# Two transformer blocks in one kernel: the square sum of the differential heads as two rounded matmuls, issued behind other matmul work

## The chip, the cores and the metric

The kernel runs on one core of one Trainium2 chip. The metric is the device time of one execution in microseconds (us), as the median of repeated runs. The profile is one execution, taken by the hardware profiler. Engines: PE (matmuls, with PEld for the load of their weights), DVE (vector), ACT (scalar), POOL (GpSimd) and SP (it issues the transfers).

## The reference

The whole is one convolution-and-attention block, followed by one block with two kinds of attention over 512 tokens of width 1024. The change lies in the second block, in the normalization of its differential heads (4 heads of width 128):

```
p = jax.nn.softmax(sc, axis=-1)
a = p[:, :, 0] - lam * p[:, :, 1]
d_out = einsum(a, dv)                                            # per head: 512 tokens x 128
d_out = rms_norm(d_out, diff_subln) * (1.0 - lambda_init)        # mean of squares over the head's 128 values
d_out = d_out * jax.nn.silu(dg)
mixed = jnp.concatenate([m_out, d_out], axis=-1)
x = x + jnp.einsum('bse,ed->bsd', mixed, w_out)
```

The other heads (`m_out`, 8 heads of width 64, handled in pairs) have a block-sparse attention of their own, which with 512 tokens is causal over all keys.

## The kernel before

Each engine has an instruction stream of its own, written out by hand in program order; semaphores join them (`wait_ge` on one side, `then_inc` on the other). An engine works through its stream in that order, so what stands behind a waiting instruction waits too.

**Precision.** A product of two fp32 matrices is done as three matmuls of rounded parts (`products`: high by high, low by high, high by low; type fp32r). ACT writes a high part, DVE or POOL the low part, which is the value minus its high part. A matmul on plain fp32 operands stands in the trace as two records, each with a weight load of its own.

**The second attention** goes over eight chunks c = 0 to 7: even ones are differential heads, odd ones are pairs of the other heads. The loop over c = 0, 2, 4, 6 interleaves the stages of c, c + 1, c + 2 and c + 3 so that PE always has projections of later chunks between the attention steps. Stages that matter here:

- `value_half(c, half)`: half of a value projection, 12 matmuls of 512 columns (L463 to L465), into PSUM bank 7. For c of 3 and more its first half waits for `v2_lo_ready`, which counts the low parts of values: `value_half(c + 3, 0)` may overwrite bank 7 only after `value_low(c + 2)` (DVE, tile `vd_lo` for an even chunk) has read it. That one waits for `stage_v2(c + 2)` on ACT (tile `vd_hi`).
- `square_out(c)` (ACT, L1537): the squares of the raw differential head, tile `d_sq`, in plain fp32.
- `square_sum(c)` (PE, L1013 and L1015): the sum of `d_sq` over the 128 values by a matmul with a matrix of ones, and then four fp32 matmuls of 128 columns that add the term for epsilon (tile `rx_d`). The result, in the output bank, is read by `variance(c)` (DVE, tile `d_v`).
- `low_probs(c + 1, 0)` (DVE, tile `pt_lo`): the low part of the transposed probabilities, 1280 columns. It reads the transposes' bank. The next ten transposes, `transposes(c + 1, 1)` (PE, L952), wait for it (`ptl_ready`), since they overwrite that bank.
- `scores2(c + 2, 0)` (PE, L928): scores of the next differential head.

In DVE's stream `value_low(c + 2)`, `variance(c)` and `low_probs(c + 1, 0)` stand one behind the other. In PE's stream the order for c = 0, 2 and 4 is: ten transposes of chunk c + 1, `square_sum(c)`, `value_half(c + 3, 0)`, `scores2(c + 2, 0)`, ten more transposes. For c = 6 the square sum is followed by `out_chunks(0, 0, 6)`, 18 matmuls of the output projection, and then by the ten transposes `transposes(7, 1)`. So the square sum stands in the program four times.

Of the kernel before, what the change touches and what calls it, by code (L numbers as in the profile page):

```python
# [8 lines left out]
F32R = mybir.dt.float32r  # L9
BF16 = mybir.dt.bfloat16  # L10
ALU = mybir.AluOpType
ACT = mybir.ActivationFunctionType
AX = mybir.AxisListType

P = 128
T = 512
D = 1024
KC = D // P
# [62 lines left out]
def two_layer_block(nc, xT, vecs, wstream, outT):  # L81
    with ExitStack() as ctx:
        at = {}
# [11 lines left out]
        def sem(name):  # L95
            return ctx.enter_context(nc.semaphore(name))
# [120 lines left out]
        s2 = put("s2", [P, 2, 1280], F32)  # L217
        v_t = put("v_t", [P, T], F32)
        d_v = put("d_v", [P, T], F32)
        rx_d = put("rx_d", [P, TB, P], F32)  # L220
        rx_m = put("rx_m", [P, TB, P], F32)
        pt_hi = put("pt_hi", [P, 1280], F32R)
# [24 lines left out]
        def out_weights(t):  # L247
# [47 lines left out]
        out_read, raw_copied, dsq_ready, dss_ready, dvar_ready, drs_ready, d_final, att2_final, mixed_ready = (  # L295
            sem("out_read"), sem("raw_copied"), sem("dsq_ready"), sem("dss_ready"), sem("dvar_ready"),
            sem("drs_ready"), sem("d_final"), sem("att2_final"), sem("mixed_ready"))
        pool_held, gap_zeroed = sem("pool_held"), sem("gap_zeroed")
        first_done, first_sq, first_acc, first_drained = (
            sem("first_done"), sem("first_sq"), sem("first_acc"), sem("first_drained"))  # L300
# [159 lines left out]
        def _(pe):  # L460
# [421 lines left out]
            def value_half(c, half):  # L882

                if c >= KC:
                    return
                n = v_unit(c)
                if half == 0:
                    if c < 2:
                        pe.wait_ge(tile_drained, CREDIT + T_Q2 + 15 + c)
                    elif c == 2:  # L890
                        pe.wait_ge(g_drained, 1)
                    else:
                        pe.wait_ge(v2_lo_ready, c)
                    pe.wait_ge(lo_ready, n + 1)
                for k in range(4 * half, 4 * half + 4):
                    w = slice(k * P, (k + 1) * P)
                    mm = products(ps[:, v_bank(c), :], w_hi[:, n % 2, w], w_lo[:, n % 2, w], a_hi[:, k, :], a_lo[:, k, :],
                                  first=k == 0, last=k == KC - 1)
                if half:
                    mm.then_inc(units_done, 1)  # L900
# [32 lines left out]
            def transposes(c, head=0):  # L933

                if c >= KC:
                    return
                tq = tq_of(c, head)
                if tq == 0:
                    pe.wait_ge(nb_used, 16)
                if is_diff(c):  # L940
                    pe.wait_ge(p2_joined, c // 2 + 1)
                    if c:
                        pe.wait_ge(row2_used, c // 2)
                else:
                    pe.wait_ge(p2_exp, 2 * c + head + 1)
                if tq:
                    pe.wait_ge(ptl_ready, tq)
                for j in range(TB):
                    for b in range(j, TB):
                        src = S_COL[b] + j * P  # L950
                        o = PT_BANK * 512 + P_COL[j] + (b - j) * P
                        mm = pe.transpose(psf[:, o:o + P], s2[:, head, src:src + P], ident[:, :])  # L952
                mm.then_inc(pt_ready, 1)
# [53 lines left out]
            def square_sum(c):  # L1007

                if c >= KC:
                    return  # L1010
                pe.wait_ge(dsq_ready, c // 2 + 1)
                pe.wait_ge(rx_ready, c + 1)
                pe.matmul(ps[:, OUT_BANK, :], ones[:, :], d_sq[:, :], start=True, stop=False, skip_group_check=True)  # L1013
                for b in range(TB):
                    mm = pe.matmul(ps[:, OUT_BANK, b * P:(b + 1) * P], rx_d[:, b, :], ident[:, :], start=False,  # L1015
                                   stop=b == TB - 1, skip_group_check=True)
                mm.then_inc(dss_ready, 1)

            def out_chunks(t, first, last):

                high, low = out_weights(t)
                if first == 0:
                    pe.wait_ge(lo_ready, U_W2 + t + 1)
                for n in range(first, last):
                    pe.wait_ge(mixed_ready, n + 1)
                    j = W2_ORDER[n]
                    w = slice(j * P, (j + 1) * P)
                    mm = products(ps[:, W2_BANKS[t], :], high[:, w], low[:, w], b_hi[:, j, :], b_lo[:, j, :],
                                  first=n == 0, last=n == KC - 1)
                if last == KC:  # L1030
                    mm.then_inc(units_done, 1)
# [34 lines left out]
            for c in range(0, KC, 2):  # L1066
                transposes(c)
                if c:
                    value_transposes(c + 1)
                scores2(c + 1, 0)  # L1070
                if 0 < c < KC - 2:
                    value_half(c + 2, 0)
                    value_half(c + 2, 1)
                    scores2(c + 1, 1)
                    gate_half(c + 1, 0)
                    scores2(c + 1, 2)
                    gate_half(c + 1, 1)
                else:
                    gate_half(c + 1, 0)
                    scores2(c + 1, 1)  # L1080
                    gate_half(c + 1, 1)
                    scores2(c + 1, 2)
                values2(c)
                value_transposes(c + 2)
                transposes(c + 1, 0)
                if c + 2 < KC:
                    square_sum(c)
                    value_half(c + 3, 0)
                    scores2(c + 2, 0)
                    transposes(c + 1, 1)  # L1090
                    scores2(c + 2, 1)
                    value_half(c + 3, 1)
                    scores2(c + 2, 2)
                    values2(c + 1, 0)
                    gate_part(c + 2, 0, 5)
                    values2(c + 1, 1)
                    den_rows(c + 1)
                    gate_part(c + 2, 5, KC)

            square_sum(KC - 2)  # L1100
            pe.wait_ge(g_drained, KC)
            out_chunks(0, 0, KC - 2)
            transposes(KC - 1, 1)
            values2(KC - 1, 0)
            pe.wait_ge(s2_biased, 4 * 16)
# [15 lines left out]
        def _(act):  # L1121
# [412 lines left out]
            def square_out(c):  # L1534

                act.wait_ge(raw_copied, c // 2 + 1)
                act.activation(d_sq[:, :], att2[:, 0, :], ACT.Square).then_inc(dsq_ready, 1)  # L1537

            def first_root(c):
# [110 lines left out]
        def _(dve):  # L1650
# [497 lines left out]
            def value_low(c):  # L2148

                if c >= KC:  # L2150
                    return
                dve.wait_ge(v2_hi_ready, c + 1)
                src = ps[:, v_bank(c), :].rearrange("p (b f) -> p b f", f=P)
                if is_diff(c):
                    low(vd_lo[:, :, :], src, vd_hi[:, :, :]).then_inc(v2_lo_ready, 1)
                else:
                    low(by_heads(v2_lo[:, :, :])[:, :, 0:3:2, :], by_heads(src), by_heads(v2_hi[:, :, :])[:, :, 0:3:2, :]
                        ).then_inc(v2_lo_ready, 1)
# [102 lines left out]
            def raw_out(c):  # L2261
# [5 lines left out]
                    dve.wait_ge(mixed_ready, c - 1)  # L2267
                dve.tensor_copy(att2[:, 0, :], ps[:, OUT_BANK, :]).then_inc(raw_copied, 1)

            def variance(c):  # L2270

                dve.wait_ge(dss_ready, c // 2 + 1)
                ts(d_v[:, :], ps[:, OUT_BANK, :], 1.0 / P, ALU.mult).then_inc(dvar_ready, 1)
# [44 lines left out]
            for c in range(0, KC, 2):  # L2318
                biased(c + 1, 0)
                low_probs(c)  # L2320
                if c:
                    value_drain(c + 2)
                den_small(c)
                den_spread(c)
                biased(c + 1, 1)
                if 0 < c < KC - 2:
                    biased(c + 1, 2)
                    gate2_drain(c + 1)
                else:
                    gate2_drain(c + 1)  # L2330
                    biased(c + 1, 2)
                raw_out(c)
                den_small(c + 1)
                den_spread(c + 1)
                slopes(c + 2)
                value_low(c + 2)
                variance(c)
                low_probs(c + 1, 0)
                biased(c + 2, 0)
                biased(c + 2, 1)  # L2340
                value_drain(c + 3)
                root(c)
                biased(c + 2, 2)
                low_probs(c + 1, 1)
                joined(c + 2, (3, 2, 0, 1))
                gate_row(c + 1)
                gate2_drain(c + 2)
                slopes(c + 3)
                value_low(c + 3)
                if c + 2 < KC:  # L2350
                    gated(c + 1)
# [355 lines left out]
```

## Time and profile before

| what | value |
|---|---|
| median of three runs | 1017.15 us (1017.1 to 1017.25) |
| the profiled execution's own time | 1017.32 us |
| span of the profiled execution | 1015.2 us |
| PE busy | 1002.7 us, 99% of the span |
| DVE, ACT, POOL busy | 557.7, 454.0, 502.3 us |
| granted clock of PE, mean | 1.0 |

The span runs from the first to the last instruction in the profile; 2.1 us of the execution lie around it. Matmul records overlap, since a matmul's record runs on while the next one is started: the distance from start to start is what one costs PE. A row of the timeline can stand for several like instructions (x10).

### The profile page before, as it was taken

How to read it: one execution, taken by the hardware profiler on the slowest of the kernel's cores; microseconds unless marked ns; L12 is line 12 of the kernel's file. 1: busy time of each engine (PE TensorE's matmuls, PEld its weight loads, DVE VectorE, ACT ScalarE, POOL GpSimd, SP SyncE). 2: the span in 40 equal slices, each digit the busy share in tenths (PEclk: the TensorE clock that was granted, in tenths of full speed). 3: DMA queues.
4: the chain of work that ended last, by engine and by line, in shares of the span. 5: the costliest groups of instructions: out<-in, count | busy, mean ns of one | idle time of the engine just before them, and what ended most of it. 6: DMA issues, size and time to landing. Idle time of an engine off the chain costs nothing.

```text
span 1015.2 us, 13705 instructions
## 1 busy us (share of the span) xinstructions
PE 1002.7 (99%) x5051; PEld 836.2 (82%) x5051; DVE 557.7 (55%) x943; ACT 454.0 (45%) x682; POOL 502.3 (49%) x296
## 2 busy tenths in 40 slices
PE   9999999999999999999999999999999999999998
PEld 7888888788888988888888888889988778777787
DVE  6799897886633964434434410116714276675731
ACT  7222346888643533323323322233554347667630
POOL 4444365742347034444444365453377544755562
PEclk9999999999999999999999999999999999999999
DMA  7232222212144022222322333333132120111112
GB/s 258 83 104 97 92 83 71 75 63 83 65 184 146 21 93 94 103 92 94 103 92 94 103 104 104 104 122 107 43 104 82 63 84 22 64 63 43 42 63 83
DMA packets 26402, 91.11 MB, mean 90 GB/s; under 512 B 3056, under 2 KB 3184, under 8 KB 26224
## 3 DMA queue, kind: packets, MB, share of 16 engines
q1 hardware_dynamic: 26352, 90.42, 26.2%
q8 instruction: 34, 0.56, 0.2%
q14 instruction: 16, 0.13, 0.0%
HBM read 88.31 MB, written 2.10 MB: 89 GB/s over the span
## 4 chain that ended last, share of the span: by engine, by line
PE 87%; DVE 7%; ACT 3%; issue 1%; DMA 1%; POOL 0%; SPq 0%; DVEq 0%; ACTq 0%
PE ps L463 27%; PE ps L464 26%; PE ps L465 26%; PE ps L928 2%; PE ps L952 1%; DVE resid L2015 1%; PE ps L622 1%; DVE a_lo L1666 1%; DMA w_raw<-weights 1%; DVE sq_x L1659 1%; DVE q_raw L1659 1%; DVE mix L1659 1%; DVE b_lo L1666 1%; ACT s L1510 0%; PE ps L638 0%
## 5 line engine op out<-in xcount | busy, mean ns | idle before, releaser
L2363 POOL TENSOR_TENSOR w_lo<-w_raw,w_hi 128x1024 fp32r<-128x1024 f32 x137 | 325.9, 2379 | 412.0 <-ACT w_hi L1129 359.2
L1129 ACT ACTIVATE w_hi<-w_raw 128x1024 fp32r<-128x1024 f32 x133 | 139.2, 1046 | 281.6 <-PE ps L465 281.6
L463 PE MATMUL ps<-a_hi,w_hi 128*128 128x512 f32 (+1 forms) x544 | 211.7, 389 | 4.2 <-DVE v_lo L1663 3.1
L465 PE MATMUL ps<-a_hi,w_lo 128*128 128x512 f32 (+1 forms) x544 | 207.0, 380 | 0.0
L464 PE MATMUL ps<-a_lo,w_hi 128*128 128x512 f32 (+1 forms) x544 | 206.9, 380 | 0.0
L463 PE MATMUL ps<-b_hi,w_hi 128*128 128x512 f32 x392 | 152.9, 390 | 0.0
L465 PE MATMUL ps<-b_hi,w_lo 128*128 128x512 f32 x392 | 152.6, 389 | 0.0
L464 PE MATMUL ps<-b_lo,w_hi 128*128 128x512 f32 x392 | 152.5, 389 | 0.0
L463 PEld LDWEIGHTS ps<-a_hi,w_hi 128*128 128x128 f32 x544 | 102.3, 188 | 27.3 <-DVE v_lo L1663 4.4
L465 PEld LDWEIGHTS ps<-a_hi,w_lo 128*128 128x128 f32 x544 | 102.3, 188 | 20.0
L464 PEld LDWEIGHTS ps<-a_lo,w_hi 128*128 128x128 f32 x544 | 102.4, 188 | 18.3 <-issue 0.2
L463 PEld LDWEIGHTS ps<-b_hi,w_hi 128*128 128x128 f32 x392 | 73.6, 188 | 15.2
L465 PEld LDWEIGHTS ps<-b_hi,w_lo 128*128 128x128 f32 x392 | 73.6, 188 | 15.2
L464 PEld LDWEIGHTS ps<-b_lo,w_hi 128*128 128x128 f32 x392 | 73.6, 188 | 15.1
L1743 DVE SCALAR_TENSOR_TENSOR ps<-u_pad,vec,ps 128x512 f32<-128x512 f32 x112 | 75.4, 750 | 0.0
L463 PE MATMUL ps<-h_hi,w_hi 128*128 128x512 f32 (+1 forms) x186 | 69.2, 372 | 0.0
L464 PE MATMUL ps<-h_lo,w_hi 128*128 128x512 f32 (+1 forms) x186 | 69.0, 371 | 0.0
L465 PE MATMUL ps<-h_hi,w_lo 128*128 128x512 f32 (+1 forms) x186 | 69.0, 371 | 0.0
L1659 DVE TENSOR_TENSOR up_h<-up_u,up_s 128x512 f32<-128x512 f32 x22 | 51.2, 2330 | 21.2 <-ACT up_s L1389 21.1
L1659 DVE TENSOR_TENSOR up_u<-ps,scale_row 128x512 f32<-128x512 f32 x22 | 15.2, 690 | 82.0 <-PE ps L465 82.0
L1659 DVE TENSOR_TENSOR sq_f<-sq_f 128x512 f32<-128x512 f32 x13 | 12.5, 960 | 82.7 <-ACT sq_f L1413 82.0
L1510 ACT ACTIVATE s<-s,smax 128x384 f32<-128x384 f32 (+2 forms) x64 | 35.2, 552 | 16.9 <-DVE smax L2188 16.9
(339 smaller groups left out, 1729.0 us busy)
## 6 DMA issues: line engine op xcount, KB each, us to landing
w_raw<-weights SPq DMA_DIRECT2D x156, 512.0 KB, 3.2
resid<-x_t SPq DMA_DIRECT2D x8, 256.0 KB, 6.7
w_raw<-weights SPq DMA_DIRECT2D x8, 256.0 KB, 6.8
resid<-x_t SPq DMA_DIRECT2D x1, 2048.0 KB, 8.7
out_t<-out_sb SPq DMA_DIRECT2D x8, 256.0 KB, 2.0
vec<-vecs SPq DMA_DIRECT2D x1, 220.0 KB, 7.1
vec<-vecs SPq DMA_DIRECT2D x1, 4.0 KB, 1.8
```

The costliest lines, as they stand in the source:

```text
L463: pe.matmul(out, s_hi, m_hi, start=first, stop=False, skip_group_check=True)
L464: pe.matmul(out, s_hi, m_lo, start=False, stop=False, skip_group_check=True)
L465: return pe.matmul(out, s_lo, m_hi, start=False, stop=last, skip_group_check=True)
L622: pe.matmul(z_of(h)[:, o:o + (b + 1) * P], q[r, tok], k[r, keys], start=b != 0 and t == 0, stop=False, skip_group_check=True)
L928: mm = pe.matmul(scores_of(part, head, b), q2[rows, tok], k2[rows, keys], start=n == 0 and t == 0, stop=False, skip_group_check=True)
L952: mm = pe.transpose(psf[:, o:o + P], s2[:, head, src:src + P], ident[:, :])
L1129: act.activation(w_hi[:, k % 2, 0:width], w_raw[:, k, 0:width], ACT.Copy).then_inc(hi_ready, 1)
L1510: e = act.activation(s2[:, head, w], s2[:, head, w], ACT.Exp, scale=-1.0, bias=smax[:, head, b:b + 1], accum_out=den[:, kind_of(c), half_o ...
L1659: return dve.tensor_tensor(out, in0, in1, op)
L1666: return dve.scalar_tensor_tensor(out=out, in0=in0, scalar=scale, in1=high.bitcast(F32), op0=ALU.mult, op1=ALU.subtract)
L1743: V.do(dve.scalar_tensor_tensor(out=acc if k == TAPS - 1 else part, in0=src, scalar=w, in1=part, op0=ALU.mult, op1=ALU.add))
L2363: pool.tensor_tensor(w_lo[:, k % 2, 0:width], w_raw[:, k, 0:width], w_hi[:, k % 2, 0:width].bitcast(F32), ALU.subtract).then_inc(lo_ready, 1)
```

## The change

- ACT squares the head twice: once into a rounded high part (`d_hi`, type fp32r, which lies where `d_v` lies), and once in fp32 as before. `d_hi` comes first.
- DVE computes the low part `d_lo` (it lies where `d_y` lies) from the two, between `value_low(c + 2)` and `variance(c)`.
- PE sums by two fp32r matmuls, ones by `d_hi` and ones by `d_lo`, in place of the fp32 one. They wait for the low part. The four matmuls of the epsilon term stay.
- In the loop `value_half(c + 3, 0)` stands ahead of `square_sum(c)`, and behind the loop `out_chunks(0, 0, 6)` stands ahead of `square_sum(6)`.

```diff
+        d_hi = place("d_hi", [P, T], F32R, at["d_v"])
+        d_lo = place("d_lo", [P, T], F32R, at["d_y"])
...
+        dsq_hi, dsq_lo = sem("dsq_hi"), sem("dsq_lo")
...
-                pe.wait_ge(dsq_ready, c // 2 + 1)
+                pe.wait_ge(dsq_lo, c // 2 + 1)
                 pe.wait_ge(rx_ready, c + 1)
-                pe.matmul(ps[:, OUT_BANK, :], ones[:, :], d_sq[:, :], start=True, stop=False, skip_group_check=True)
+                pe.matmul(ps[:, OUT_BANK, :], ones[:, :].bitcast(F32R), d_hi[:, :], start=True, stop=False, skip_group_check=True)
+                pe.matmul(ps[:, OUT_BANK, :], ones[:, :].bitcast(F32R), d_lo[:, :], start=False, stop=False, skip_group_check=True)
...
                 if c + 2 < KC:
+                    value_half(c + 3, 0)
                     square_sum(c)
-                    value_half(c + 3, 0)
                     scores2(c + 2, 0)
                     transposes(c + 1, 1)
...
-            square_sum(KC - 2)
             pe.wait_ge(g_drained, KC)
             out_chunks(0, 0, KC - 2)
+            square_sum(KC - 2)
             transposes(KC - 1, 1)
...
                 act.wait_ge(raw_copied, c // 2 + 1)
+                act.activation(d_hi[:, :], att2[:, 0, :], ACT.Square).then_inc(dsq_hi, 1)
                 act.activation(d_sq[:, :], att2[:, 0, :], ACT.Square).then_inc(dsq_ready, 1)
...
+            def square_low(c):
+
+                dve.wait_ge(dsq_hi, c // 2 + 1)
+                dve.wait_ge(dsq_ready, c // 2 + 1)
+                low(d_lo[:, :], d_sq[:, :], d_hi[:, :]).then_inc(dsq_lo, 1)
...
                 value_low(c + 2)
+                square_low(c)
                 variance(c)
                 low_probs(c + 1, 0)
```

How the instructions stand, engine by engine. On PE in the loop's first pass (c = 0), behind the matmuls of the attention's values: `s` are the exponentials that the transposes turn, `w` and `a` the value projection's weights and activations, `k` and `q` the scores' operands. Before:

```order
L952 MATMUL ps<-ident,s_126 128x128 [waits ptl_ready,p2_exp]
L952 MATMUL ps<-ident,s_126 128x128 x9
L1013 MATMUL ps<-d_sq,ones 128x512 [waits rx_ready,dsq_ready]
L1015 MATMUL ps<-ident,rx_d 128x128 x4
L463 MATMUL ps<-a_hi,w_hi 128x512 [waits lo_ready,v2_lo_ready]
L464 MATMUL ps<-a_lo,w_hi 128x512
L465 MATMUL ps<-a_hi,w_lo 128x512
...
L465 MATMUL ps<-a_hi,w_lo 128x512
L928 MATMUL ps<-k_hi,q_hi 128x512 [waits s2_biased,qk2_lo]
...
L952 MATMUL ps<-ident,s_126 128x128 [waits ptl_ready,p2_exp]
```

and now:

```order
L955 MATMUL ps<-ident,s_126 128x128 [waits ptl_ready,p2_exp]
L955 MATMUL ps<-ident,s_126 128x128 x9
L466 MATMUL ps<-a_hi,w_hi 128x512 [waits lo_ready,v2_lo_ready]
L467 MATMUL ps<-a_lo,w_hi 128x512
...
L468 MATMUL ps<-a_hi,w_lo 128x512
L1016 MATMUL ps<-d_hi,ones 128x512 [waits rx_ready,dsq_lo]
L1017 MATMUL ps<-d_lo,ones 128x512
L1019 MATMUL ps<-ident,rx_d 128x128 x4
L931 MATMUL ps<-k_hi,q_hi 128x512 [waits s2_biased,qk2_lo]
...
L955 MATMUL ps<-ident,s_126 128x128 [waits ptl_ready,p2_exp]
```

The twelve matmuls of the value half, with their wait on `v2_lo_ready`, have gone ahead of the sum, and the sum stands directly ahead of the scores and of the next transposes with their wait on `ptl_ready`.

On DVE in the same pass, behind the copy of the raw head. Before:

```order
L2232 COPY rx_m<-den 128x512 [waits nb_used,vec_step]
L1655 TENSOR_SCALAR bias_h<-dist,small 128x512 [waits s2_biased]
L1663 TENSOR_TENSOR vd_lo<-ps,vd_hi 128x512 [waits v2_hi_ready]
L1655 TENSOR_SCALAR d_v<-ps 128x512 [waits dss_ready]
L1663 TENSOR_TENSOR pt_lo<-ps,pt_hi 128x1280 [waits pth_ready]
L2185 MEMSET small 128x1 [waits pt_ready,s2_ready,vec_step]
L2188 ISA s_126,smax<-ps,bias_h 128x512
```

and now:

```order
L2237 COPY rx_m<-den 128x512 [waits nb_used,vec_step]
L1660 TENSOR_SCALAR bias_h<-dist,small 128x512 [waits s2_biased]
L1668 TENSOR_TENSOR vd_lo<-ps,vd_hi 128x512 [waits v2_hi_ready]
L1668 TENSOR_TENSOR d_lo<-d_sq,d_hi 128x512 [waits dsq_ready,dsq_hi]
L1660 TENSOR_SCALAR d_v<-ps 128x512 [waits dss_ready]
L1668 TENSOR_TENSOR pt_lo<-ps,pt_hi 128x1280 [waits pth_ready]
L2190 MEMSET small 128x1 [waits pt_ready,s2_ready,vec_step]
L2193 ISA s_126,smax<-ps,bias_h 128x512
```

One subtraction has come in ahead of the variance; the variance, which waits for PE's sum (`dss_ready`), still stands ahead of `pt_lo`.

On PE behind the loop (c = 6), `b` and `w` being the output projection's operands. Before:

```order
L952 MATMUL ps<-ident,s_126 128x128 [waits ptl_ready,p2_exp]
L952 MATMUL ps<-ident,s_126 128x128 x9
L1013 MATMUL ps<-d_sq,ones 128x512 [waits rx_ready,dsq_ready]
L1015 MATMUL ps<-ident,rx_d 128x128 x4
L463 MATMUL ps<-b_hi,w_hi 128x512 [waits mixed_ready,lo_ready,g_drained]
...
L465 MATMUL ps<-b_hi,w_lo 128x512
L952 MATMUL ps<-ident,s_126 128x128 [waits ptl_ready,p2_exp]
```

and now:

```order
L955 MATMUL ps<-ident,s_126 128x128 [waits ptl_ready,p2_exp]
L955 MATMUL ps<-ident,s_126 128x128 x9
L466 MATMUL ps<-b_hi,w_hi 128x512 [waits mixed_ready,lo_ready,g_drained]
...
L468 MATMUL ps<-b_hi,w_lo 128x512
L1016 MATMUL ps<-d_hi,ones 128x512 [waits rx_ready,dsq_lo]
L1017 MATMUL ps<-d_lo,ones 128x512
L1019 MATMUL ps<-ident,rx_d 128x128 x4
L955 MATMUL ps<-ident,s_126 128x128 [waits ptl_ready,p2_exp]
```

The 18 output matmuls stand ahead of the sum now, and the transposes that wait on `ptl_ready` directly behind it.

## Rows read from the trace of the kernel before

**Rows 1.** Page, part 1: busy us, share of span, instructions of each engine.
```profile
PE 1002.7 (99%) x5051; PEld 836.2 (82%) x5051; DVE 557.7 (55%) x943; ACT 454.0 (45%) x682; POOL 502.3 (49%) x296
```

**Rows 2.** Waits of PE from 800 us on: total, times, longest.
```profile
PE ps L463 <- DVE v_lo L1663: 3.1, 3, 1.0
PE ps L1013 <- ACT d_sq L1537: 0.3, 1, 0.3
```

**Rows 3.** Timeline, PE, first pass: start, duration (us), line, operation.
```profile
841.34 1.26 PE L952 MATMUL ps<-ident,s 128*128 128x128 f32 x10
842.49 1.12 PE L1013 MATMUL ps<-d_sq,ones 128*128 128x512 f32 x2
843.45 1.05 PE L1015 MATMUL ps<-ident,rx_d 128*128 128x128 f32 x8
844.26 0.48 PE L463 MATMUL ps<-a_hi,w_hi 128*128 128x512 f32 x1
...
846.88 0.39 PE L465 MATMUL ps<-a_hi,w_lo 128*128 128x512 f32 x1
847.20 0.50 PE L928 MATMUL ps<-k_hi,q_hi 64*128 64x512 f32 x2
...
848.09 1.31 PE L952 MATMUL ps<-ident,s 128*128 128x128 f32 x10
```

**Rows 4.** Timeline, DVE, the same stretch.
```profile
842.95 0.69 DVE L1663 TENSOR_TENSOR vd_lo<-ps,vd_hi 128x512 fp32r<-128x512 f32 x1
844.54 0.69 DVE L1655 TENSOR_SCALAR d_v<-ps 128x512 f32<-128x512 f32 x1 [0.90 <-PE ps L1015]
845.15 1.48 DVE L1663 TENSOR_TENSOR pt_lo<-ps,pt_hi 128x1280 fp32r<-128x1280 f32 x1
848.28 0.06 DVE L2185 MEMSET small<- 128x1 f32 x1 [1.65 <-issue]
```

**Rows 5.** Timeline, ACT, the same stretch.
```profile
841.80 0.63 ACT L1537 ACTIVATE d_sq<-att 128x512 f32<-128x512 f32 x1 [0.55 <-DVE att L2268]
842.34 0.58 ACT L1497 ACTIVATE vd_hi<-ps 128x512 fp32r<-128x512 f32 x1
```

**Rows 6.** Timeline, second pass: ACT, DVE, then two rows of PE.
```profile
883.67 0.58 ACT L1497 ACTIVATE vd_hi<-ps 128x512 fp32r<-128x512 f32 x1
...
884.80 0.68 DVE L1663 TENSOR_TENSOR vd_lo<-ps,vd_hi 128x512 fp32r<-128x512 f32 x1
...
885.59 0.47 PE L463 MATMUL ps<-a_hi,w_hi 128*128 128x512 f32 x1
...
889.41 1.31 PE L952 MATMUL ps<-ident,s 128*128 128x128 f32 x10
```

**Rows 7.** Timeline, PE, last pass.
```profile
959.37 1.28 PE L952 MATMUL ps<-ident,s 128*128 128x128 f32 x10
960.98 1.12 PE L1013 MATMUL ps<-d_sq,ones 128*128 128x512 f32 x2 [0.33 <-ACT d_sq L1537]
...
962.75 0.47 PE L463 MATMUL ps<-b_hi,w_hi 128*128 128x512 f32 x1
...
966.96 1.25 PE L952 MATMUL ps<-ident,s 128*128 128x128 f32 x10
967.97 0.48 PE L463 MATMUL ps<-pt_hi,v_hi 128*128 128x512 f32 x1
```

**Rows 8.** Timeline of the later wait, all engines.
```profile
864.00 4.91 POOL L2363 TENSOR_TENSOR w_lo<-w_raw,w_hi 128x1024 fp32r<-128x1024 f32 x2
864.49 2.18 DVE L1655 TENSOR_SCALAR bias<-dist,small 128x512 f32<-128x512 f32 x1
...
867.32 0.50 PE L463 MATMUL ps<-a_hi,w_hi 128*128 128x512 f32 x1 [1.03 <-DVE v_lo L1663]
```

**Rows 9.** Tile d_sq: one operation, duration ns min/median/max.
```profile
L1659 DVE TENSOR_TENSOR d_sq<-d_y x4: 681/681/2117, 854.0 to 966.1; 128x512 f32<-128x512 f32 x4
```

**Rows 10.** Stretch 860 to 870: busy us, granted clock (PEclk), DMA.
```profile
860.00:870.00 10.00, 8.97 (x55) 7.43 (x54) 7.95 (x15) 4.89 (x8) 8.78 (x8) 1.00 0.17 54
```


## The prediction

> **What bounds the kernel now.** I read the page first: PE is busy for 1002.7 of 1015.2 us [rows 1], so a microsecond that PE gains or loses is one of the result, unless PE waits nearby for something that was late anyway. Then the waits of PE from 800 us on, where all of the change lies: PE waits three times for a `v_lo`, 3.1 us in all, and once for `d_sq`, 0.3 us [rows 2]. Then the timelines of PE, DVE and ACT around the square sum [rows 3 to 5]. There are two things to see. The sum costs PE 1.77 us, from 842.49 to 844.26, of which the fp32 matmul takes 0.96 (842.49 to 843.45, two passes) and the epsilon term 0.81. And it costs nothing, because the next instruction, the value half, could not have started earlier: it overwrites what `vd_lo` reads, and `vd_lo` ends at 842.95 + 0.69 = 843.64. In the second pass the cover is exact: `vd_lo` ends at 884.80 + 0.68 = 885.48 and the value half starts at 885.59 [rows 6]. So the sum stands in the shadow of DVE's `vd_lo`, and behind it the value half (2.85 us) and the scores (0.89) give DVE the time for `d_v` and `pt_lo`, which are done at 845.15 + 1.48 = 846.63, well ahead of the transposes at 848.09 that wait for `pt_lo`.
>
> **The sum itself.** Two fp32r matmuls replace the fp32 one. Their price is the pitch of such matmuls: 18 of them take 962.75 to 966.96, 0.23 us each [rows 7]. So 0.47 in place of 0.96: 0.49 less PE work, four times, 1.96 us in all. That is the gain if the order costs nothing.
>
> **ACT.** One more square, ahead of `d_sq`. From `d_sq` to `vd_hi` ACT takes 0.54 (841.80 to 842.34) [rows 5], so `vd_hi` comes 0.54 later: 842.88 to 843.46 in the first pass. `vd_lo` follows 0.03 behind (842.92 to 842.95 now), at 843.49, and ends at 844.18. In the second pass `vd_hi` moves to 884.21 and ends at 884.79; `vd_lo`, which DVE started at 884.80 for reasons of its own, moves by some 0.02 [rows 6]. What stands behind on ACT (`pt_hi`, the gate) comes 0.54 later too and isn't awaited for microseconds.
>
> **DVE.** One more subtraction, `d_lo`, from SBUF to SBUF. The nearest row is `d_sq<-d_y`, of the same shape and place: 0.68 us, and 2.12 where POOL was in its way [rows 9]. From 844.18 that ends between 844.8 and 846.3. Both lie ahead of the sum's new time (847.1, below), so it costs nothing. If the cover went, it would be 0.6 to 2.1 per pass.
>
> **The order on PE, passes c = 0, 2 and 4.** Now the value half is first, and PE comes to it when the ten transposes are issued: 841.34 + 1.01 (what ten of them take ahead of full matmuls, 966.96 to 967.97) = 842.35. It waits for `vd_lo` until 844.18, and 0.06 more (`d_sq` ended at 842.43, and its matmul began at 842.49). So it starts at 844.24, where it started before (844.26), and PE has idled for 1.9 us in which the sum used to run. Then, step by step:
> - value half, 844.24 + 2.85 (844.26 to 846.88, and one pitch) = 847.09;
> - the sum's two matmuls, 0.47: the epsilon term starts at 847.56;
> - `d_v` starts 1.09 behind that start, as now (843.45 to 844.54): 848.65;
> - `pt_lo` starts 0.61 behind (844.54 to 845.15) and takes 1.48: done at 850.74;
> - the transposes start 0.06 later: 850.80. Now they start at 848.09. The pass loses 2.71 us.
>
> In between PE has the epsilon term (0.81) and the scores (0.89), so it comes to the transposes at about 849.3 and waits 1.5 us. The whole of `d_v` and `pt_lo` lay under the value half and lies bare now. In the second pass the same steps from 885.56 give 892.12, against 889.41: again 2.71. The third pass repeats the second.
>
> What is late next: the scores' bias on DVE stands behind `pt_lo`. DVE idled 1.65 ahead of it (848.28) [rows 4], so it starts at about 850.7 rather than 848.28, less late than PE. The transposes set the pace of what follows, and all of it moves by 2.71.
>
> **The last pass, c = 6.** PE comes to the output matmuls at 959.37 + 1.01 = 960.38; it no longer waits for `d_sq` (0.33). They take 4.21, to 964.59. The sum's 0.47, then 1.09, 0.61, 1.48 and 0.06 lead to 968.30 for the transposes, against 966.96 [rows 7]: 1.34 lost. The 4.21 us of output matmuls used to cover `d_v` and `pt_lo` (2.09).
>
> **The sum.** 3 x 2.71 + 1.34 = 9.5 us. The profiled execution took 1017.32 (span 1015.2 and 2.1 around it), so 1026.8; it stands 0.17 above the median, and against the median it is **1026.6 us**.
>
> **Bounds.** The switch from rounded to plain fp32 matmuls is not in the trace in this place; it could add up to 0.14, by which ten transposes take longer ahead of the fp32 sum (841.34 to 842.49, 1.15) than ahead of rounded matmuls (1.01), or nothing: +0.6 over four. I take nothing, since the 1.15 may hold a short wait for `d_sq`. The 0.06 and 0.03 of handing over may be 0.1 each: +0.5. On the low side the work behind may take some back (below).
>
> **A rule that speaks against more.** PE's granted clock is 1.00 in the stretch that holds a wait of 1.03 [rows 8, 10], the full of its two levels. The new waits are 1.9 and 1.5 us with 5 us of work between. By the Trainium skill ("TensorE: Matmul & The Clock Gate", "HAM oscillation — how this bites in real kernels") bursts of matmuls between waits can put the clock to its half again and again. No run here shows that yet, and the row speaks against it; the sum goes by the full clock.
>
> **Rivals.**
> - *A part is given back.* The later wait of 1.03 in each pass hangs on `bias`, which takes 2.18 us beside POOL's `w_lo` [rows 8]. If POOL, not delayed as much as DVE, were past that by then, the wait would go: 3 x 1.03 = 3.1 back, 1023.5. The Trainium skill ("GPSIMD Engine Reference", table of specifications) says that POOL shares its SBUF access with such DVE instructions, which would make this a matter of timing. Against it: the weights that POOL splits there wait for PE's own progress. Chance 0.09.
> - *Only the first wait.* If `pt_lo` did not stand behind `d_v`, PE would lose only what the sum takes after the half, 0.47 + 0.81 = 1.28, per pass, and gain 0.33 + 0.49 = 0.82 in the last: +3.0, 1020.2. The order on DVE speaks against it. Chance 0.04.
> - *Faster.* If the new order cost nothing, the sum's 1.96 and the wait of 0.33 would be saved: 1014.9. For that `pt_lo` must be done when PE comes to the transposes. It decides at 848.0: later than that, a pass loses. By the rows `pt_lo` alone takes 1.48, so it would have to start at 846.5, ahead of the end of the value half that now stands ahead of its sum. Chance 0.05.
> - *The clock falls.* If the 5.0 us of work between the two waits (2.85, 0.47, 0.81, 0.89) ran at half the clock in three passes, 15 us more: 1042. Chance 0.02.
> - *Both effects small*, the waits and the saving, so that they cancel: within 0.2% (2 us, about what a measurement of this kernel can tell from no change). Chance 0.02.
>
> **The numbers.** The forecast, slower by 9.5, has 0.78. The range goes from the first rival, with some margin (1023.0), to the forecast plus its upper bounds of 1.1 and as much margin as below (1028.2); it leaves out the others and the forecast's own misses, some 0.17. Slower: 0.78 + 0.09 + 0.04 + 0.02 = 0.93; same 0.02; faster 0.05.
>
> **What the profile after would show.** Right: PE waits some 1.9 us for `vd_lo` ahead of a value half and some 1.5 us for `pt_lo` ahead of ten transposes, three times each; in the last pass it waits for `pt_lo` alone (from 965.06 + 0.81 = 965.87 to 968.30: 2.4). The ones matmuls have a pitch of 0.23. `d_v` waits for PE longer than now (0.90). Wrong: if no wait on `vd_lo` shows, the first step fails; if `pt_lo` ends before PE gets to the transposes, the second; if the waits for `v_lo` are gone, the first rival is at work; if PE's clock is below 1.00 from 840 us on, the fourth.

## The result, and the profile after

The changed kernel takes 1028.62 us (median of five executions, 1026.84 to 1028.65) against 1017.15: slower by 11.5 us. The ratio over all executions is 1.0104 [1.0094, 1.0115]; the two medians alone give 1.0113. The forecast was 1026.6, slower, with a range up to 1028.2: the direction and the mechanism came, and the median lies 0.4 us above the range. The five executions stand at two levels, 1028.62 to 1028.65 three times, with a mean granted clock of 0.998, and 1026.84 and 1026.85 twice, with 1.0. The lower level is the forecast to 0.3 us; the 1.8 us between them is told below. The profile is of an execution of the upper level, with a span of 1026.5 us (before 1015.2).

The page's first part, and the waits of PE from 800 us on (total, times, longest):

```profile
PE 1002.1 (98%) x5051; PEld 837.3 (82%) x5051; DVE 559.2 (54%) x947; ACT 456.2 (44%) x686; POOL 503.3 (49%) x296
```

```profile
PE ps L955 <- DVE pt_lo L1668: 6.4, 4, 2.3
PE ps L466 <- DVE vd_lo L1668: 4.9, 3, 1.6
PE ps L466 <- DVE v_lo L1668: 3.2, 3, 1.1
```

PE is busy for about as long as before [rows 1], in a span 11.3 us longer. Seven waits are new, four on `pt_lo` and three on `vd_lo`, 11.3 us in all (the 2 us of work saved and what the clock takes below nearly cancel); the one on `d_sq` is gone, and the three on `v_lo` stand as they did [rows 2]. PE's timeline of the first pass (start, duration, operation, idle time ahead of it and what ended it) answers to [rows 3]:

```profile
841.34 1.25 PE L955 MATMUL ps<-ident,s 128*128 128x128 f32 x10
...
844.22 0.49 PE L466 MATMUL ps<-a_hi,w_hi 128*128 128x512 f32 x1 [1.62 <-DVE vd_lo L1668]
...
847.05 0.40 PE L1016 MATMUL ps<-d_hi,ones 128*128 128x512 f32 x1
847.29 0.40 PE L1017 MATMUL ps<-d_lo,ones 128*128 128x512 f32 x1
...
850.86 1.28 PE L955 MATMUL ps<-ident,s 128*128 128x128 f32 x10 [1.38 <-DVE pt_lo L1668]
```

The value half starts at 844.22, where it started before (844.26), and the time in which the sum used to run lies empty. The transposes start at 850.86, 2.77 later than at 848.09. ACT and DVE in the same stretch, answering to [rows 4, 5]:

```profile
841.81 0.63 ACT L1541 ACTIVATE d_hi<-att 128x512 fp32r<-128x512 f32 x1 [0.55 <-DVE att L2273]
842.35 0.61 ACT L1542 ACTIVATE d_sq<-att 128x512 f32<-128x512 f32 x1
842.87 0.58 ACT L1501 ACTIVATE vd_hi<-ps 128x512 fp32r<-128x512 f32 x1
843.34 1.23 ACT L1526 ACTIVATE pt_hi<-ps 128x1280 fp32r<-128x1280 f32 x1
```

```profile
843.47 0.69 DVE L1668 TENSOR_TENSOR vd_lo<-ps,vd_hi 128x512 fp32r<-128x512 f32 x1 [0.67 <-ACT vd_hi L1501]
844.08 0.68 DVE L1668 TENSOR_TENSOR d_lo<-d_sq,d_hi 128x512 fp32r<-128x512 f32 x1
848.62 0.69 DVE L1660 TENSOR_SCALAR d_v<-ps 128x512 f32<-128x512 f32 x1 [3.86 <-PE ps L1019]
849.23 1.48 DVE L1668 TENSOR_TENSOR pt_lo<-ps,pt_hi 128x1280 fp32r<-128x1280 f32 x1
```

`vd_hi` is 0.53 later, behind the second square, and `vd_lo` 0.52. DVE is through with `d_lo` at 844.76 and then stands still for 3.86 us at `d_v`; `pt_lo`, whose high part was done at 844.57 (843.34 + 1.23), stands behind it. The second and third pass repeat this: their transposes start at 894.96 and 939.06, 5.55 and 8.33 behind those of before (889.41 [rows 6] and 930.73), 2.78 more with each pass. Now:

```profile
894.96 1.28 PE L955 MATMUL ps<-ident,s 128*128 128x128 f32 x10 [1.38 <-DVE pt_lo L1668]
...
939.06 1.28 PE L955 MATMUL ps<-ident,s 128*128 128x128 f32 x10 [1.38 <-DVE pt_lo L1668]
```

and before, in the third pass:

```profile
930.73 1.31 PE L952 MATMUL ps<-ident,s 128*128 128x128 f32 x10
```

In the last pass they start at 976.70 against 966.96, 9.74 behind, so that pass loses 1.41:

```profile
976.70 1.28 PE L955 MATMUL ps<-ident,s 128*128 128x128 f32 x10 [2.27 <-DVE pt_lo L1668]
```

Behind that wait PE's clock falls. The stretches of 2 us (PE's busy time, the other engines', then the granted clock, PEclk):

```profile
976.00:978.00 2.00, 1.30 (x11) 1.33 (x12) 2.00 (x4) 1.94 (x4) 0.41 (x1) 0.97 0.18 20
978.00:980.00 2.00, 2.00 (x6) 1.71 (x6) 1.16 (x2) 0.33 (x1) 0.66 (x1) 0.50 0.64 250
980.00:982.00 2.00, 2.00 (x11) 1.87 (x11) 0.00 (x0) 0.50 (x1) 1.86 (x2) 0.68 0.00 0
```

The matmuls behind these transposes take 3.46 us (977.74 to 981.20) where they took 1.95 (967.97 [rows 7] to 969.92). Now, and then before:

```profile
977.74 0.67 PE L466 MATMUL ps<-pt_hi,v_hi 128*128 128x512 f32 x1
...
981.20 0.49 PE L466 MATMUL ps<-b_hi,w_hi 128*128 128x512 f32 x1
```

```profile
969.92 0.45 PE L463 MATMUL ps<-b_hi,w_hi 128*128 128x512 f32 x1
```

So 9.74 for the waits, net of what the split saves, and 1.5 for the clock make up the 11.3.

### The profile page after: what moved, and what is told of

It is laid out like the page before. It is cut to its first block, busy times and chain, and to the rows that moved or that the text cites. A ratio compares the mean times of both kernels' runs of the same rounds, so it can differ in the third digit from the quotient of the medians.

```text
span 1026.5 us, 13717 instructions
## 1 busy us (share of the span) xinstructions
PE 1002.1 (98%) x5051; PEld 837.3 (82%) x5051; DVE 559.2 (54%) x947; ACT 456.2 (44%) x686; POOL 503.3 (49%) x296
## 4 chain that ended last, share of the span: by engine, by line
PE 86%; DVE 8%; ACT 3%; issue 1%; DMA 1%; POOL 0%; SPq 0%; DVEq 0%; ACTq 0%
PE ps L466 27%; PE ps L468 26%; PE ps L467 26%; PE ps L931 2%; PE ps L955 1%; DVE resid L2020 1%; PE ps L625 1%; DVE a_lo L1671 1%; DMA resid<-x_t 1%; DVE sq_x L1664 1%; DVE q_raw L1664 1%; DVE mix L1664 1%; DVE b_lo L1671 1%; DVE pt_lo L1668 0%; ACT s L1514 0%
```

## The experiments

Code differences are against the changed kernel unless something else is said. Ratios are against the kernel before on the same chip, whose median there is given with the first run of each group. A pass is counted from its first ten transposes to its second; before it takes 6.75 us (841.34 to 848.09) and the last one 7.59 (959.37 to 966.96) [rows 3, 7], and what a pass loses or gains is against these. So counted, the change's passes lose 2.77, 2.80, 2.80 and 1.43.

**The two halves of the change** (before: 1017.12). The split with the old order on PE:

```diff
-                    value_half(c + 3, 0)
                     square_sum(c)
+                    value_half(c + 3, 0)
...
+            square_sum(KC - 2)
             pe.wait_ge(g_drained, KC)
             out_chunks(0, 0, KC - 2)
-            square_sum(KC - 2)
```

> The split alone: two rounded matmuls, the second square on ACT and the subtraction on DVE as in the change, and both orders on PE as before. Theory (the order costs, by two waits): the sum now waits for d_lo. In the first pass d_lo ends at about 844.8 where d_sq was ready at 842.4, so the sum runs from 844.8 to 846.1 and the value half starts 1.8 us later than before; pt_lo is done well ahead of the transposes. In the last pass the sum waits some 1.2 us and saves 0.5: 0.7 lost. In all 3 x 1.8 + 0.7 = 6.2 slower: 1023.4, with no wait on pt_lo and none on vd_lo. Rival (the split is what costs in the change, through the added work on ACT and DVE): as slow as the change, 1026.8. Rival (the split is all gain): 1015.2.

It took 1028.02 (1027.84 to 1028.05), 1.0107 [1.0091, 1.0122]: no better than the whole change: the number of the first rival (1026.8) and not of the theory (1023.4). Its wait on `d_lo` and the two `d_lo` of the first and second pass:

```profile
PE ps L1016 <- DVE d_lo L1668: 9.2, 4, 2.7
```

```profile
844.07 0.68 DVE L1668 TENSOR_TENSOR d_lo<-d_sq,d_hi 128x512 fp32r<-128x512 f32 x1
...
888.97 1.14 DVE L1668 TENSOR_TENSOR d_lo<-d_sq,d_hi 128x512 fp32r<-128x512 f32 x1
```

The first wait is 2.22, and the sum starts at 844.81, as worked out; the second wait is 2.68, since `d_lo` takes 1.14 beside POOL, and the third pass is like it. Around the first two waits the clock halves; behind the third it doesn't (last line):

```profile
846.00:848.00 2.00, 2.00 (x9) 1.81 (x9) 0.77 (x2) 1.97 (x4) 1.52 (x2) 0.50 0.00 0
...
890.00:892.00 2.00, 1.84 (x6) 1.65 (x7) 0.11 (x1) 1.96 (x3) 2.00 (x3) 0.50 0.00 0
...
936.00:938.00 2.00, 2.00 (x15) 1.79 (x14) 1.01 (x2) 1.97 (x4) 2.00 (x3) 1.00 0.00 0
```

The passes lose 3.54, 3.83, 2.40 and 0.92. The third, with a wait as long as the second's but the clock at 1.00, shows the price without the clock. So the kind of loss was as worked out: no wait on `pt_lo` or `vd_lo` is left, and all of it hangs on `d_lo`. Its size was not, because of `d_lo` beside POOL and of the clock. In the change PE never waits for `d_lo`, so this loss is no part of the change's 11.5.

The order alone, with the sum in plain fp32, as edited in the kernel before:

```diff
+                    value_half(c + 3, 0)
                     square_sum(c)
-                    value_half(c + 3, 0)
...
-            square_sum(KC - 2)
             pe.wait_ge(g_drained, KC)
             out_chunks(0, 0, KC - 2)
+            square_sum(KC - 2)
```

> The order alone: the plain fp32 sum of before, without d_hi and d_lo, behind the value half in the loop and behind the 18 output matmuls after it. Theory: the value half waits for vd_lo until 843.7, the sum follows at 846.6 with 0.96 for its matmul, and the transposes wait for pt_lo until about 850.8: 2.7 lost per pass; 1.8 in the last, where the sum's matmul is 0.49 longer than in the change. In all 9.8 slower: 1027.0, and 1.8 more in executions in which PE's clock falls to the half in the last pass. Rival (the split costs): about 1017, or 2 to 3 us slower at most.

1028.06 (1027.9 to 1029.4), 1.0112 [1.0096, 1.0127]. Its waits are those of the change:

```profile
PE ps L952 <- DVE pt_lo L1663: 6.4, 4, 2.3
PE ps L463 <- DVE vd_lo L1663: 4.3, 3, 1.6
```

The passes lose 2.65, 3.18, 3.18 and 1.82, 10.8 in all; the second and third lose 0.5 more than worked out, since `vd_lo` is held there by DVE's own `rx_m` and not by ACT. In the second pass (ACT, then DVE):

```profile
886.18 0.58 ACT L1497 ACTIVATE vd_hi<-ps 128x512 fp32r<-128x512 f32 x1
```

```profile
885.76 1.24 DVE L2232 COPY rx_m<-den 128x512 f32<-128x512 f32 x1
...
887.31 0.68 DVE L1663 TENSOR_TENSOR vd_lo<-ps,vd_hi 128x512 fp32r<-128x512 f32 x1
```

Behind its wait of 2.27 the clock stays at 1.00:

```profile
978.00:980.00 2.00, 2.00 (x16) 1.87 (x15) 1.97 (x4) 1.25 (x2) 0.00 (x0) 1.00 0.59 223
```

The order alone is enough for the whole loss, and makes it by the change's own two waits. Either half alone costs as much as both: each puts PE in front of an operand that isn't there yet, but not the same one, so the two losses don't add. At full clock the change is some 1.2 us faster than this kernel (1026.84 against 1027.99, the middle one of its three executions with a mean clock of 1.0): inside the new order the split does save some 0.4 in each of the last three passes.

**Each wait by itself.** The change with `pt_lo` ahead of `d_v` on DVE:

```diff
                 square_low(c)
-                variance(c)
                 low_probs(c + 1, 0)
+                variance(c)
```

> The change, with one line moved on DVE: the low part of the probabilities (pt_lo) ahead of the variance (d_v). Theory: the wait on vd_lo stays (1.6 us, three times), the wait of the transposes on pt_lo goes. A pass then loses what the sum takes behind the value half, 0.47 + 0.81 and a little for the switch, 1.3 to 1.4; the last pass gains 0.8. In all 3.1 to 3.4 slower: 1020.4, and PE's clock stays at its full level. Rival (the second wait is only a symptom, and PE waits somewhere else instead, for d_v or the scores' bias): 1024 to 1027.

1020.85 (1020.69 to 1021.14), 1.0037 [1.0023, 1.0051]. That is the price of the rival *only the first wait* (1020.2). No wait on `pt_lo` is left; those on `vd_lo` stand (4.9, 3 times). The passes lose 1.32, 1.35 and 1.36, and the last gains 1.0, of which PE gives 0.3 back at the first output weights:

```profile
PE ps L466 <- POOL wo_lo L2576: 0.3, 1, 0.3
```

So `d_v` ahead of `pt_lo` is the cause of the second wait, and it was worth 7.8 of the 11.5 us, the clock's part included.

The change with the last sum in its old place, ahead of the output matmuls:

```diff
+            square_sum(KC - 2)
             pe.wait_ge(g_drained, KC)
             out_chunks(0, 0, KC - 2)
-            square_sum(KC - 2)
```

> The change, with the order behind the loop as before (the last sum ahead of the 18 output matmuls). Theory: the three passes lose 2.77 each as in the change; the last sum waits for d_lo and loses 0.7. In all 9.0 slower: 1026.2. The fall of PE's clock comes from the wait of 2.3 us in the last pass; that wait is gone here, so all executions agree and the clock is full throughout. Rival (the clock falls because of the shorter waits as well): two levels of time again, some 1.8 apart, or half clock somewhere in the loop.

1026.57 (1026.13 to 1026.94), 1.0094 [1.0079, 1.0110], with a mean clock of 1.0 in every execution. Its waits are 4.9 on `vd_lo`, 4.1 on `pt_lo` (three times each) and one of 1.6 on `d_lo`. With the wait of 2.27 gone, the fall of the clock is gone. Four executions are few to show it, though: `e2_order_only` keeps the wait, and the mean clock is below 1.0 in only one of its four (0.998, in the one of 1029.4).

**What the added work costs where nothing reads it** (before: 1017.16 and 1017.11). `d_hi` and `d_lo` are computed, the sum is the plain one in its old place, and the output does not depend on them:

```diff
-                pe.wait_ge(dsq_lo, c // 2 + 1)
+                pe.wait_ge(dsq_ready, c // 2 + 1)
...
-                pe.matmul(ps[:, OUT_BANK, :], ones[:, :].bitcast(F32R), d_hi[:, :], start=True, stop=False, skip_group_check=True)
-                pe.matmul(ps[:, OUT_BANK, :], ones[:, :].bitcast(F32R), d_lo[:, :], start=False, stop=False, skip_group_check=True)
+                pe.matmul(ps[:, OUT_BANK, :], ones[:, :], d_sq[:, :], start=True, stop=False, skip_group_check=True)
...
                 dve.wait_ge(dss_ready, c // 2 + 1)
+                dve.wait_ge(dsq_lo, c // 2 + 1)
```

> The added work alone: ACT writes d_hi and DVE d_lo as in the change (the variance waits for d_lo, so that its tile is free), but nothing reads d_lo: PE sums the plain fp32 squares in the order of before. Theory (the work itself is free, only who waits for it costs): vd_lo ends 0.54 later, at the time at which the sum ends; d_v starts at most 0.4 later and pt_lo is still ahead of its transposes. 0 to 0.5 slower in all, 1017.1 to 1017.6. Rival (the added work on ACT and DVE carries part of the loss): 2 us or more.

1019.19 (1018.94 to 1019.61), 1.0020 [1.0011, 1.0029]: 2.0 slower where 0 to 0.5 was expected, as its rival said. `d_hi` stands ahead of `d_sq` on ACT, and the plain sum waits for `d_sq` four times:

```profile
PE ps L1016 <- ACT d_sq L1541: 2.1, 4, 0.8
```

The same with `d_hi` behind `d_sq` and `vd_hi` on ACT, against `e5_idle_parts`:

```diff
-                act.activation(d_hi[:, :], att2[:, 0, :], ACT.Square).then_inc(dsq_hi, 1)
                 act.activation(d_sq[:, :], att2[:, 0, :], ACT.Square).then_inc(dsq_ready, 1)
...
                 square_out(c)
                 stage_v2(c + 2)
+                square_high(c)
```

> e5_idle_parts with d_hi behind d_sq and vd_hi on ScalarE: d_hi and d_lo are computed and nothing reads them, the sum is the plain one in its old place, the output is as before. Theory: the two added operations cost nothing where they stand behind what TensorE waits for; the 2.0 that e5_idle_parts lost were the square's delay alone: 1017.1 to 1017.6. Rival: the added work costs by VectorE's and POOL's contention wherever it stands: as e5_idle_parts, 1019.2.

1016.91 (1016.44 to 1017.14), 0.9998 [0.9989, 1.0007]. The added work is free; its place on ACT was the cost.

**Both engines' streams turned to fit the order** (before: 1017.16). The values' parts ahead of the squares on ACT and directly behind the raw copy on DVE, and `pt_lo` ahead of `d_v`:

```diff
-                square_out(c)
                 stage_v2(c + 2)
+                square_out(c)
...
                 raw_out(c)
+                value_low(c + 2)
                 den_small(c + 1)
                 den_spread(c + 1)
                 slopes(c + 2)
-                value_low(c + 2)
                 square_low(c)
-                variance(c)
                 low_probs(c + 1, 0)
+                variance(c)
```

> The change, with the order on ACT and DVE made to fit it: vd_hi ahead of the two squares on ACT; on DVE vd_lo directly behind the copy of the raw head, and pt_lo ahead of the variance. Theory (the loss is two waits, so it goes with them): the value half starts at about 842.9 and the scores at about 847.2, as before the change; the last pass gains 1.0. 1016.2 in all, 1.0 faster than before, and PE waits for neither pt_lo nor, by more than 0.5, vd_lo. Rival (the reordering only moves the loss): 1018 or more.

1018.77 (1018.51 to 1019.15), 1.0016 [1.0007, 1.0025]: a part of the loss has moved, as the rival said. The passes lose 0.02, 1.10 and 1.06, and the last gains 1.0. In the second pass DVE meets POOL twice (first DVE, then POOL):

```profile
883.04 0.69 DVE L1668 TENSOR_TENSOR vd_lo<-ps,vd_hi 128x512 fp32r<-128x512 f32 x1 [0.40 <-ACT vd_hi L1501]
...
883.88 1.56 DVE L2237 COPY rx_m<-den 128x512 f32<-128x512 f32 x1
...
885.75 1.77 DVE L1668 TENSOR_TENSOR d_lo<-d_sq,d_hi 128x512 fp32r<-128x512 f32 x1
887.45 1.48 DVE L1668 TENSOR_TENSOR pt_lo<-ps,pt_hi 128x1280 fp32r<-128x1280 f32 x1
```

```profile
883.86 1.29 POOL L2534 TENSOR_TENSOR q_lo<-y_qk,q_hi 128x512 fp32r<-128x512 f32 x1
...
885.44 1.54 POOL L2534 TENSOR_TENSOR k_lo<-y_qk,k_hi 128x512 fp32r<-128x512 f32 x1
887.10 1.58 POOL L2554 TENSOR_TENSOR gate_e<-gate_g,gate_e 128x512 f32<-128x512 f32 x1
```

`rx_m` begins with POOL's `q_lo` and takes 1.56 (0.78 in the first pass), `d_lo` lies beside `k_lo` and takes 1.77 (0.68). PE waits 0.8 for `d_lo` in these two passes. By the Trainium skill ("GPSIMD Engine Reference", table of specifications) POOL shares its SBUF interfaces with DVE instructions that have two SBUF inputs, as `d_lo` has; the 1.77 agrees.

The same, with the epsilon term's matmuls ahead of the value half and of the output matmuls, so that only the two ones matmuls stay behind; against `b1_values_first`:

```diff
...
+                    epsilon_part(c)
                     value_half(c + 3, 0)
                     square_sum(c)
...
+            epsilon_part(KC - 2)
             pe.wait_ge(g_drained, KC)
             out_chunks(0, 0, KC - 2)
```

> The kernel b1, with the epsilon term's four matmuls ahead of the value half (and ahead of the 18 output matmuls), where they fill what is left of the wait on vd_lo; only the two rounded matmuls stay behind. Theory: a pass has 0.81 less behind the half and starts the half some 0.35 later: about 0.6 faster per pass than before, 1.0 in the last: 1014.5. Rival (PE finds no idle time there to fill): as b1, 1016.2.

1016.60 (1016.05 to 1016.9), 0.9995 [0.9986, 1.0004]. The passes: -0.56, +0.17, +0.19, -1.01. The first and the last are as worked out; the second and third still wait 0.5 for `d_lo` and gain nothing, which is most of the 2.1 us between the forecast and the result. And that with the plain sum in place of the split, `d_hi` and `d_lo` left out:

```diff
-                pe.wait_ge(dsq_lo, c // 2 + 1)
-                pe.matmul(ps[:, OUT_BANK, :], ones[:, :].bitcast(F32R), d_hi[:, :], start=False, stop=False, skip_group_check=True)
-                mm = pe.matmul(ps[:, OUT_BANK, :], ones[:, :].bitcast(F32R), d_lo[:, :], start=False, stop=True, skip_group_check=True)
+                pe.wait_ge(dsq_ready, c // 2 + 1)
+                mm = pe.matmul(ps[:, OUT_BANK, :], ones[:, :], d_sq[:, :], start=False, stop=True, skip_group_check=True)
```

> The kernel b2 with the plain fp32 sum of before in place of the two rounded matmuls, and without d_hi and d_lo. It tells what the split is worth where nothing waits for it. Theory: 0.49 more PE time in each of four places, 2.0 slower than b2: 1016.5. Rival (the split gains nothing, since PE waits elsewhere for what it saves): as b2.

1016.74 (1016.26 to 1017.06), 0.9995 [0.9986, 1.0004]. The passes: -0.18, -0.16, -0.17, -0.62. With the order cured, the split gains 0.4 in the first and in the last pass and loses 0.3 to 0.4 in each of the other two; in all it is worth nothing that can be measured.

`d_lo` ahead of what meets POOL, against `b2_epsilon_ahead` (before: 1017.11):

```diff
                 value_low(c + 2)
+                square_low(c)
+                low_probs(c + 1, 0)
                 den_small(c + 1)
                 den_spread(c + 1)
                 slopes(c + 2)
-                square_low(c)
-                low_probs(c + 1, 0)
                 variance(c)
```

> b2_epsilon_ahead with VectorE's stream after the raw copy in the order vd_lo, d_lo, pt_lo, then the reciprocal sums, rx_m and the bias, then d_v. Theory: in the second and third pass TensorE waits for d_lo only because rx_m and the bias stand ahead of it there beside POOL's work; with d_lo ahead of them the wait of 0.5 in two passes goes, each pass ends 0.56 earlier than before the change, the last 1.0 earlier, and w_lo of the next stage gives 0.3 back: 1017.15 - 3 x 0.56 - 1.0 + 0.3 = 1014.8, 2.0 below b3_plain_sum (1016.74). Rival: the contention of VectorE with POOL only moves on, onto the bias or d_v, and something behind them (the scores of the next unit, pt_lo) waits in d_lo's place: as b2_epsilon_ahead, 1016.6.

1024.20 (1023.53 to 1025.16), 1.0072 [1.0058, 1.0085], worse than both said. The four passes do gain what was worked out (-0.56, -0.56, -0.56 and -1.01), and no wait on `d_lo` is left, but the scores behind them wait for `smax`, which needs the bias that was pushed back. The wait, DVE in the second pass, and POOL beside it:

```profile
PE ps L931 <- DVE smax L2199: 5.8, 3, 2.8
```

```profile
884.59 1.54 DVE L1674 TENSOR_TENSOR d_lo<-d_sq,d_hi 128x512 fp32r<-128x512 f32 x1 [0.41 <-ACT d_sq L1548]
886.05 1.48 DVE L1674 TENSOR_TENSOR pt_lo<-ps,pt_hi 128x1280 fp32r<-128x1280 f32 x1
...
887.67 1.46 DVE L2243 COPY rx_m<-den 128x512 f32<-128x512 f32 x1
889.05 2.59 DVE L1666 TENSOR_SCALAR bias_h<-dist,small 128x512 f32<-128x512 f32 x1
```

```profile
888.79 2.56 POOL L2381 TENSOR_TENSOR w_lo<-w_raw,w_hi 128x1024 fp32r<-128x1024 f32 x1
```

From 884.59 to 891.64 DVE has no gap. The rival's mechanism is shown, at a price that neither named: the bias, 0.47 us in the change's first pass, takes 2.59 beside POOL here, and behind the third pass's wait of 2.73 the clock falls to 0.50, which costs 2.9 more (second transposes of the third pass to those of the last: 40.80 us against 36.23 before, of which the wait of 2.73 and the gain of 1.01 leave 2.85):

```profile
936.00:938.00 2.00, 1.50 (x12) 1.50 (x12) 1.07 (x5) 1.52 (x5) 0.35 (x1) 0.50 0.81 266
```

Last, `b2_epsilon_ahead` with the split in the first and last pass alone (before: 1017.41):

```diff
+                if 0 < c < KC - 2:
+                    pe.wait_ge(dsq_ready, c // 2 + 1)
+                    mm = pe.matmul(ps[:, OUT_BANK, :], ones[:, :], d_sq[:, :], start=False, stop=True, skip_group_check=True)
+                    mm.then_inc(dss_ready, 1)
+                    return
...
-                square_low(c)
+                if not 0 < c < KC - 2:
+                    square_low(c)
```

> b2_epsilon_ahead with the split in the first and the last pass alone, where d_lo is in time there; the second and third pass sum d_sq in one plain fp32 matmul as b3_plain_sum does, and neither d_hi nor d_lo is made in them. Theory: the passes keep what they showed apart: 0.56 earlier in the first (b2_epsilon_ahead), 0.16 each in the second and third (b3_plain_sum), 1.0 in the last (b2_epsilon_ahead), and w_lo of the next stage gives 0.3 back: 1017.15 - 0.56 - 0.32 - 1.0 + 0.3 = 1015.6, faster than both kernels. Rival: a pass that ends earlier meets the next one's VectorE work and waits there, so nothing is left: as b2_epsilon_ahead and b3_plain_sum, 1016.7.

1016.23 (11 of 12 executions from 1015.79 to 1017.52; one took 3533.75, and one of the kernel before 5137.66; the medians hardly move by them), 0.9990 [0.9981, 0.9999]. The passes came as expected, -0.56, -0.16, -0.17 and -1.01, 1.9 in all; the last one's transposes:

```profile
958.60 1.28 PE L955 MATMUL ps<-ident,s 128*128 128x128 f32 x10
...
965.18 1.25 PE L955 MATMUL ps<-ident,s 128*128 128x128 f32 x10
```

They begin at 965.18, 1.78 ahead of before. Some of it is given back behind (0.3 at `wo_lo`), and the medians differ by 1.2. It has the lowest ratio of the study, but its interval overlaps those of `b2_epsilon_ahead` and `b3_plain_sum`, so it is not shown to be faster than these two; and it only just leaves out no change from the kernel before.

## Why the prediction was right, and where it was off

- **The sum stood in the shadow of `vd_lo`, and the value half would not start earlier for being first.** Right: 844.22 (forecast 844.24, before 844.26). PE's idle time was forecast as 1.9 and shows as 1.62, since the transposes' records run on after the next could start.
- **`d_v` and `pt_lo` lie bare behind the moved sum.** Right: `d_v` 848.62 (848.65), transposes 850.86 (850.80), 2.77 to 2.78 a pass (2.71). The missing 0.06 lies in the last step: the transposes start 0.15 behind the end of `pt_lo` (850.71), where 0.06 was taken. `e3_probs_first` shows that `d_v` ahead of `pt_lo` is the cause of this wait, and `e2_order_only` that it comes from the order without the split.
- **ACT's square delays `vd_hi` by 0.54.** Right for the first pass (0.53); in `e2_order_only`, without it, PE waits 0.5 less for `vd_lo` there (1.11 against 1.62). In the second and third pass it decides nothing: PE waits 1.61 without it and 1.62 with it.
- **The last pass.** 1.41 against a forecast of 1.34, with a wait of 2.27 (2.4).
- **The saving of 0.49 a pass.** The pitch (start to start) is right: 847.05 to 847.29, 0.24. The saving is some 0.4 rather than 0.49, since behind rounded matmuls the plain fp32 one takes 0.86 (846.41 to 847.27 in `e2_order_only`) and not 0.96: from the value half's start to the transposes the change's first pass takes 6.64 us (844.22 to 850.86) and `e2_order_only` 7.04 (843.56 to 850.60), and `b3_plain_sum` against `b2_epsilon_ahead` shows 0.38 and 0.39 in the passes where `d_lo` is in time.
- **`d_lo` costs nothing under cover, 0.6 to 2.1 without.** Right under cover. `e1_split_only`, where the cover is gone, waits 2.2 to 2.7 for it in the loop, since `d_lo` also stands behind `vd_lo`.
- **"The sum goes by the full clock"** is the step that was off, in one place. The argument weighed the new waits of 1.9 and 1.5 and left out the longest, the 2.4 that the same prediction forecast for the last pass. The rival of a falling clock was priced as three passes of halved work, 15 us, and given 0.02; the sum had no term for one fall. What came was one fall, behind the last pass's wait, of 1.5 us in the profile (1.8 between the two levels of the executions), in three executions of five. That is what put the median above the range. By the prediction's own sign, a clock below 1.00 from 840 us on, its fourth rival was at work, in a tenth of its size. `e4_loop_only` removes that wait and the fall with it. The row that was taken as evidence [rows 8, 10] was of a wait of 1.03, less than half of this one. By the Trainium skill ("TensorE: Matmul & The Clock Gate", "HAM oscillation — how this bites in real kernels") a matmul kernel can find the clock halved behind each of its waits; the trace agrees for the wait of 2.27 and not for those of 1.62 and 1.38, behind which the clock stayed at 1.00.
- **Part given back**: did not happen; the waits on `v_lo` are 3.2 in all, before 3.1.

## What to carry to other kernels

Work that stands ahead of a waiting instruction may be free where it stands: before moving it, ask whether what then comes first could have started earlier, and what stands behind the moved work's consumer on the other engines' streams, since those are in order too. In this kernel the new order on PE cost nothing only once ACT's and DVE's orders were turned to match it, and where DVE's stretch was already full, each rearrangement shifted the wait on to the next operand. Splitting the matmul into rounded parts paid only where the low part was ready without anyone waiting for it.

## What the runs showed of the hardware that was not expected

- The granted clock fell to 0.50 around some single waits of 2.2 to 2.7 us (2.27 in the change, 2.22 and 2.68 in `e1_split_only`, 2.73 in `b4_low_parts_first`), but not all such waits: behind 2.68 in `e1_split_only`'s third pass, 2.27 in `e2_order_only` and 2.76 in `b4_low_parts_first` it stayed at 1.00. Behind waits up to 1.65 it fell in none of the profiled executions. One fall cost 1.4 us (second pass of `e1_split_only`, 3.83 against the third's 2.40) to 2.9. What decides between the cases is open.
- The same DVE operation on 128x512 takes between 0.68 and 1.77 (`d_lo`), 0.43 and 1.56 (`rx_m`), and 0.47 and 2.59 (the bias), and the long ones lie beside work of POOL. So the same instruction costs two and a half to five and a half times as much when a rearrangement of DVE's stream brings it there. The three longest began just behind an operation of POOL and ended 0.3 to 0.5 us behind its end: `d_lo` at 887.52 with `k_lo` done at 886.98, `rx_m` at 885.44 with `q_lo` at 885.15 (both in `b1_values_first`), the bias at 891.64 with `w_lo` at 891.35 (`b4_low_parts_first`). So each seems to have spent most of its time waiting for POOL's operation to end; no run tests this. `pt_lo`, which reads one operand from PSUM, took its 1.48 beside POOL's `gate_e` too.
